# ScalarE's order in a state-space loop, and where the loop's preparation stands, in a two-layer hybrid decoder step

## The reference, cut to what matters

```python
def s5_mixer(n, x0_re, x0_im, a_re, a_im, log_dt, b_re, b_im, c_re, c_im, d, w_glu):
    dt = jnp.exp(log_dt)[:, None]
    mag = jnp.exp(a_re * dt)
    lr = mag * jnp.cos(a_im * dt)
    li = mag * jnp.sin(a_im * dt)
    ...
    cr = ((lr - 1.0) * a_re + li * a_im) / den
    ci = (li * a_re - (lr - 1.0) * a_im) / den
    bbr, bbi = cr * b_re - ci * b_im, cr * b_im + ci * b_re
    ...
    _, _, xr, xi = lax.associative_scan(s5_combine, (ar, ai, bur, bui), axis=0)
    y = Re(C x) + d * n
    zg = jnp.einsum('bld,dz->blz', jax.nn.gelu(y), w_glu)
    return zg[..., :D_MODEL] * jax.nn.sigmoid(zg[..., D_MODEL:]), xr[-1], xi[-1]

def channel_mixer(h, g, w_up, w_down):
    a = jax.nn.relu(jnp.einsum('bld,df->blf', rmsnorm(h, g), w_up))
    return jnp.einsum('blf,fd->bld', a * a, w_down)
```

## Time and profile before

| | us |
|---|---|
| median of 3 executions | 1099.26 (1097.96 to 1101.6) |
| the profiled execution | 1100.49 |
| its span | 1098.8, mean granted TensorE clock 0.946 |
| TensorE (PE) busy | 1043.7 (95%) |
| VectorE (DVE) busy | 551.4 (50%) |
| ScalarE (ACT) busy | 414.5 (38%) |
| GpSimd (POOL) busy | 138.1 (13%) |
| up projection of layer 0 | 446 to 556 |
| state-space loop | 739 to 797 |
| gated projection | 797 to 851 |

### The profile page before, as it was taken

The page is one execution under the profiler, slowest core; times in us unless marked ns, Lnnn a source line. Parts: engine busy times, 40 slices in busy tenths (PEclk is TensorE's granted clock), DMA queues, the critical chain, the costliest instruction groups (busy, mean ns, idle before and its releaser), DMA issues.

```text
span 1098.8 us, 16432 instructions
## 1 busy us (share of the span) xinstructions
PE 1043.7 (95%) x6342; PEld 872.5 (79%) x6342; DVE 551.4 (50%) x965; ACT 414.5 (38%) x711; POOL 138.1 (13%) x236
## 2 busy tenths in 40 slices
PE   6998979999999969999999999999999999999997
PEld 5997536556665537889987777778999999999997
DVE  4441675556445234398451002349665675634454
ACT  6423343343123113357341001633456555533343
POOL 3441000000014303000031001850000000000000
PEclk9998978999789979999999999999589999999999
DMA  7447001211225423434432343031034444433341
GB/s 293 163 164 294 28 1 30 76 36 34 77 92 171 152 78 125 154 129 178 154 138 98 148 153 152 2 148 55 1 137 154 154 156 174 171 153 154 154 153 44
DMA packets 33758, 135.26 MB, mean 123 GB/s; under 512 B 5257, under 2 KB 16777, under 8 KB 21010
## 3 DMA queue, kind: packets, MB, share of 16 engines
q1 hardware_dynamic: 26786, 116.71, 29.1%
q0 software_dynamic: 6896, 17.51, 4.8%
HBM read 130.04 MB, written 4.17 MB: 122 GB/s over the span
## 4 chain that ended last, share of the span: by engine, by line
PE 77%; DVE 11%; ACT 5%; issue 4%; POOLq 1%; DMA 1%; POOL 1%; DVEq 0%; ACTq 0%
PE ps L805 17%; PE ps L774 12%; PE ps L775 12%; PE ps L776 11%; PE ps L965 8%; DVE ring_split L1728 2%; PE ps L870 1%; PE ps L968 1%; PE ps L1241 1%; POOLq L609 1%; PE ps L1030 1%; PE ps L1249 1%; PE ps L1256 1%; PE ps L1255 1%; ACT glu_hi_split L1354 1%
## 5 line engine op out<-in xcount | busy, mean ns | idle before, releaser
L965 PE MATMUL ps<-arena 128*128 128x512 f32 x256 | 147.3, 667 | 0.0
L805 PE MATMUL ps<-arena,ring 128*128 128x288 f32 x512 | 124.3, 406 | 0.0
L805 PEld LDWEIGHTS ps<-arena,ring 128*128 128x128 f32 x512 | 97.2, 190 | 26.8
L968 PEld LDWEIGHTS ps<-arena 128*128 128x128 f32 x256 | 51.0, 199 | 66.2 <-issue 66.2
L774 PE MATMUL ps<-nhi_split,hi_split 128*128 128x288 f32 x320 | 95.2, 298 | 1.7 <-DVE up_lo_split L1737 1.6
L776 PE MATMUL ps<-nhi_split,ring_split 128*128 128x288 f32 x320 | 94.1, 294 | 0.0
L1728 DVE TENSOR_TENSOR ring_split<-ring,hi_split 128x2048 fp32r<-128x2048 f32 x36 | 82.2, 2286 | 23.0 <-ACT hi_split L1354 23.0
L1861 DVE TENSOR_REDUCE arena<-arena 128x8 f32<-128x512 f32 x64 | 43.5, 684 | 78.6 <-ACT arena L1429 78.6
L774 PE MATMUL ps<-up_nhi_split,up_hi_split 128*128 128x288 f32 x256 | 76.6, 299 | 4.4 <-DVE ring_split L1728 2.4
L1354 ACT ACTIVATE hi_split<-ring 128x2048 fp32r<-128x2048 f32 x36 | 68.7, 1910 | 31.4 <-PE ps L776 22.7
L2030 DVE TENSOR_TENSOR hT<-hT,ps 128x288 f32<-128x288 f32 x24 | 10.9, 453 | 132.9 <-PE ps L805 100.8
(11 more groups left out here) (377 smaller groups left out, 2343.2 us busy)
## 6 DMA issues: line engine op xcount, KB each, us to landing
ring<-in_stream SPq DMA_DIRECT2D x97, 1024.0 KB, 4.9
arena<-in_ckvT SPq DMA_DIRECT2D x64, 128.0 KB, 2.0
arena<-in_ckv POOLq DMA_DIRECT2D x49, 128.0 KB, 2.6
arena<-in_wu POOLq DMA_DIRECT2D x1, 2176.0 KB, 10.2
arena<-in_s POOLq DMA_DIRECT2D x4, 512.0 KB, 3.8
out_gla_s<-arena POOLq DMA_DIRECT2D x4, 512.0 KB, 2.9
arena<-in_ckv SPq DMA_DIRECT2D x15, 128.0 KB, 2.3
hT<-in_x SPq DMA_DIRECT2D x2, 576.0 KB, 4.5
```

The costliest lines, as they stand in the source:

```text
L805: mm = pe.matmul(ps[base:base + m, 0:T], wv[:, k, col:col + m], rhs(k), start=first and k == 0, stop=last and k == blocks - 1)
L965: mm = pe.matmul(ps[:, :], pages[:, p % 4, j, k], wuk[:, k], start=k == 0, stop=k == KB - 1)
L968: mm = pe.matmul(sc[:, 32 * j:32 * j + 32], pages[:, p % 4, j, k], qabs[:, k, b], start=False, stop=j == 1 and k == KB - 1, skip_group_che ...
```

## The change

```diff
--- before.py
+++ after.py
@@ -213,10 +213,9 @@
                 if i >= 0:
                     g.add(("y5", i), "side", 4, 4 + turn % 4)
                     turn += 1
-            for i in range(0, 8, 2):
-                for n in (i, i + 1):
-                    main(("glu_a", n))
-                    main(("glu_g", n))
+            for n in range(8):
+                main(("glu_a", n))
+                main(("glu_g", n))
         side(("ss", 1 + 3 * L))
         for i in range(FB):
             main(("up", L, i))
@@ -1276,13 +1275,11 @@
                 for name, col in (("glu_a", 0), ("glu_g", P)):
                     project_split((name, i), w, col, 256, glu_split, wait, blocks=range(lo, hi), last=hi == DB, first=lo == 0)

-            for i in range(2):
-                pe.wait_ge(glu_first, i + 1)
-                glu_pieces(i, 0, 4, split_wait(2) if i == 0 else None)
-            for i in range(2):
-                split_unit(f"glu{i}")
-                glu_pieces(i, 4, 8, split_wait(2) if i == 0 else None)
-            for i in range(2, 8):
+            pe.wait_ge(glu_first, 1)
+            glu_pieces(0, 0, 4, split_wait(2))
+            split_unit("glu0")
+            glu_pieces(0, 4, 8, split_wait(2))
+            for i in range(1, 8):
                 split_unit(f"glu{i}")
                 glu_pieces(i, 0, 8)
             mlp(1)
@@ -1548,12 +1545,12 @@
                     hi_unit(U["up0_1"])
                 if b == 5:
                     hi_unit(U["up0_2"])
-            rsqrt(rs[:, :], ("ss", 1))
             act.wait_ge(s5_angle, 1)
             act.activation(cf(4), cf(1), ACT.Exp).then_inc(s5_sin, 1)
             act.activation(cf(5), cf(2), ACT.Sin).then_inc(s5_sin, 1)
             act.activation(cf(6), cf(2), ACT.Sin, scale=0.5).then_inc(s5_sin, 1)
             table_with_exp_and_ln()
+            rsqrt(rs[:, :], ("ss", 1))
             for i in range(6):
                 squared_up(0, i)
             act.wait_ge(s5_zero, 1)
@@ -1646,19 +1643,20 @@
                 for b in range(4 * half, 4 * half + 4):
                     act.activation(glu_nhi[:, b], n3[:, b], ACT.Copy).then_inc(n_hi, 1)

-            for i in range(-2, 8):
-                if i + 2 < 8:
-                    sample_inputs(i + 2, 0)
-                    sample_inputs(i + 2, 1)
-                    sample_states(i + 2)
-                    last_states(i + 2)
-                if i >= 0:
-                    mixed(i)
-                if i == 4:
+            for i in range(10):
+                if i < 8:
+                    sample_inputs(i, 0)
+                    sample_inputs(i, 1)
+                    sample_states(i)
+                if 1 <= i < 9:
+                    last_states(i - 1)
+                if i >= 2:
+                    mixed(i - 2)
+                if i == 6:
                     n_hi_half(0)
-                if i == 5:
+                if i == 7:
                     hi_unit(U["glu0"])
-                if i == 6:
+                if i == 8:
                     hi_unit(U["glu1"])
             n_hi_half(1)
             table_with_exp_and_ln()
@@ -2046,7 +2044,7 @@
                     dve.wait_ge(a_hi, i)
                     V.tensor_tensor(a2lo[:, i - 1], a2[:, i - 1], as_whole(a2hi[:, i - 1]), ALU.subtract).then_inc(a_split, 1)

-            def gated(base, values, gates, unit_of=None, after=None, normed=False):
+            def gated(base, values, gates, unit_of=None, between=None, after=None, normed=False):

                 for i in range(8):
                     e = (tA, tB)[(base + i) % 2]
@@ -2055,6 +2053,8 @@
                         V.tensor_tensor(e, ps[:, 0:T], rs[:, :], ALU.mult).then_inc(bank_of(gates[i]), 1)
                     if unit_of:
                         lo_unit(unit_of(i))
+                    if between:
+                        between(i)
                     ps = result(dve, values[i])
                     dve.wait_ge(gate_ready, base + i + 1)
                     V.tensor_tensor(e, e, ps[:, 0:T], ALU.mult).then_inc(bank_of(values[i]), 1)
@@ -2078,7 +2078,6 @@
                     lo_unit(U["up0_2"])
                 gained_lo(1, b, prm("g_mlp0"), up_nhi, up_lo)
             add_squares(1, 2)
-            copied(dve, ("ss", 1))

             def s5_prepare():

@@ -2098,7 +2097,6 @@
                 link(V.scalar_tensor_tensor(cf(2), cf(3), -C1, cf(2), ALU.mult, ALU.add))
                 link(V.scalar_tensor_tensor(cf(2), cf(3), -C2, cf(2), ALU.mult, ALU.add))
                 V.tensor_scalar(cf(2), cf(2), 3.1415925, -3.1415925, ALU.min, ALU.max).then_inc(s5_angle, 1)
-                up(0, range(0, 1))
                 dve.wait_ge(s5_sin, 3)
                 tt(cf(6), cf(6), cf(6), ALU.mult)
                 link(V.tensor_scalar(cf(6), cf(6), -2.0, 1.0, ALU.mult, ALU.add))
@@ -2111,16 +2109,12 @@
                     tt(pr, t0, t1, ALU.subtract)
                     tt(t0, xr, xi, ALU.mult)
                     tt(pi, t0, t0, ALU.add)
-                    if pr is l2r:
-                        up(0, range(1, 2))
-                up(0, range(2, 3))
                 for i, (x, s) in enumerate(((l4r, 1.0), (l4i, -1.0), (l4i, 1.0), (l4r, 1.0))):
                     link(V.tensor_scalar(cf(16 + i), x, s, None, ALU.mult))

                 tt(t0, are, are, ALU.mult)
                 tt(t1, aim, aim, ALU.mult)
                 tt(cf(13), t0, t1, ALU.add)
-                up(0, range(3, 4))
                 link(V.reciprocal(cf(13), cf(13)))
                 link(V.tensor_scalar(cf(14), lr, -1.0, None, ALU.add))
                 tt(t0, cf(14), are, ALU.mult)
@@ -2146,7 +2140,8 @@
                 dve.wait_ge(s5raw_in, 80)
                 tt(braw[0], braw[0], g_rows, ALU.mult)
                 tt(braw[1], braw[1], g_rows, ALU.mult)
-                up(0, range(4, 5))
+                copied(dve, ("ss", 1))
+                up(0, range(0, 5))
                 cmul(cur, braw, cf(15), cf(14), b_power, range(5, 6))
                 for e in range(1, 4):
                     up(0, range(3 + 3 * e, 5 + 3 * e))
@@ -2281,12 +2276,11 @@
             lo_half(0, 0)
             for b in range(4):
                 n_lo(2, b, glu_nhi)
-            lo_half(1, 0)
             lo_half(0, 1)
             for b in range(4, DB):
                 n_lo(2, b, glu_nhi)
-            lo_half(1, 1)
-            parts[0] += 2
+            parts[0] += 1
+            lo_unit(U["glu1"])

             def final_states():

@@ -2312,15 +2306,13 @@
             def h_lo_parts(i):
                 if i:
                     dve.wait_ge(h_gated, 8 + i)
-                    if i < 7:
-                        gained_lo(3, i - 1, prm("g_mlp1"), to=up1_lo)
+                    gained_lo(3, i - 1, prm("g_mlp1"), to=up1_lo)
                 if i in (4, 6):
                     add_squares(4, i // 2 - 2)

-            gated(8, [("glu_a", i) for i in range(8)], [("glu_g", i) for i in range(8)], unit_of=lambda i: U[f"glu{i}"] + 2, after=h_lo_parts)
-            for b in (6, 7):
-                dve.wait_ge(h_gated, 8 + b + 1)
-                gained_lo(3, b, prm("g_mlp1"), to=up1_lo)
+            gated(8, [("glu_a", i) for i in range(8)], [("glu_g", i) for i in range(8)], unit_of=lambda i: U[f"glu{i}"] + 2, between=h_lo_parts)
+            dve.wait_ge(h_gated, 16)
+            gained_lo(3, 7, prm("g_mlp1"), to=up1_lo)
             add_squares(4, 2)
             lo_unit(U["up1_0"] + 2)
             copied(dve, ("ss", 4))
```

## The result

The kernel after takes 1092.38 us (1090.19 to 1094.51, 5 executions), the kernel before 1100.12 (1097.96 to 1101.6, 5): ratio 0.9943 [0.9925, 0.9961]. The ratios, with their 95% intervals, are not the quotients of the medians (1092.38 / 1100.12 = 0.9930), so both are given. The kernel is faster, as forecast, and inside the range, but by 7.7 us between the medians (6.3 by the ratio) and not by 10.3. One execution of all that follow, 1298.96 us in e7_fill at a mean clock of 0.732, was a slow one and is left out of the ratios. The profiled execution took 1092.79, span 1091.1, mean granted clock 0.950 (before 1100.49, 1098.8, 0.946).

A forecast was written before the change was run, and what follows sets the result against it. TensorE, busy for 95% of the span, was taken to bound the kernel. The terms -3.6 - 7.9 + 1.15 = -10.3 us gave 1090.2 for a profiled execution, 1089.0 on the median's scale; range 1086 to 1097.

The forecast's parts named there:

- Part 1: Layer 0's up projection: state-space preparation ahead of the first factor's evacuations cuts TensorE's waits for VectorE; -3.6 us.
- 0.1 of restart each: Layer 0's up projection: some 0.1 us of TensorE restart saved with each wait that goes.
- Part 2: State-space loop: ScalarE's new order removes waits and the clock falls only near 774; -7.9 us.
- the wait on the samples: State-space loop: VectorE's 0.78 us wait for ScalarE's samples was to go.
- Rival (a): State-space loop: the clock still falls near 764, total gain only 3.5 us, 1095.7; chance 0.18.
- Part 3: Gated projection: unit 0 before unit 1, h's low parts ahead of the product; a loss of +1.15 us.
- The chain's own arithmetic: Gated projection: the serial ScalarE-VectorE chain takes 5.9 + 0.43 us a unit, with h's low part in it.
- the first gate: Gated projection: ready earlier because unit 0 finishes first, ending VectorE's 0.71 us wait; -0.6 us.
- longer than 1.63: Start of layer 1's first factor: TensorE's wait above 1.63 us was a sign that the forecast is right.

The follow-up runs named there:

- e7_fill: The change as made plus 3, 4 and 3 unread matmuls in TensorE's waits of the loop's last three output blocks; median 1092.92 us, ratio 0.9939.
- e2: The kernel before with only ScalarE's new order in the state-space loop; median 1096.7 us, ratio 0.9963.
- e4: The kernel before with the early preparation and the new loop order, without the gated projection's edits; median 1090.11 us, ratio 0.9888.
- e5: The change as made, unchanged, run again; median 1094.96 us, ratio 0.9952 to the kernel before.
- e6: The change as made, with h's low part moved ahead of the weight unit's low part; median 1090.17 us, ratio 0.9918 to before.
- e9: The change as made, but with h's low parts behind the addition, as in the kernel before; median 1092.46 us, ratio 0.9928 to before.
- e10: The change as made, but with the old unit order in the gated projection; median 1095.14 us, ratio 0.9953 to before.
- e12_before: The kernel before, unchanged, profiled a second time; one execution, 1098.22 us.
- e3_gated: The kernel before with only the gated projection's edits (unit order, h's low parts ahead of the product); median 1101.81 us, ratio 1.0013.
- e1_prep: The kernel before with only the state-space preparation moved ahead of layer 0's first evacuations; median 1102.35 us, ratio 1.0017.
- e8_both: The change as made, with h's low part ahead of the unit's and the unread filler matmuls; median 1086.38 us, ratio 0.9886 to before.

## Why the prediction was right or wrong

**Part 1: mechanism right, -3.6 mis-sized.** It measured -4.29 in its stage in all profiles that have it. The preparation ended 12.0 us behind its start (451.44 to 463.48), as forecast (449.2 to 461.2), and the first wait shrank from 1.48 to 1.19 (forecast 1.28). TensorE's waits fell by 3.3, forecast 3.1. What was too small is the 0.1 of restart each: 4.29 - 3.3 leaves 1.0 for four waits gone, about 0.25 each. The starts of before's matmuls show it: at the wait of 0.55 us the starts are 0.84 apart and the next start follows 0.24 later, where 0.13 is the usual distance. The table load took 1.28 us and the next operation began 0.01 behind it, and the preparation ended as the row had it, not 1.4 us later. By the Trainium skill, ScalarE: Activation LUTs, "What ACT_TABLE_LOAD costs", a drain of about 1.38 us comes with each switch; it doesn't show in this trace.

**Part 2: right for the profile, wrong for the kernel.** The step that failed is the base of the -7.9: the low clock from 764 on the earlier trace rows is charged to the kernel before as if every execution had it, and only some do. Against that profile -7.9 was forecast and -7.98 measured, with the clock up to 774, the wait on the samples gone and VectorE at 5.39 us a block, as written. But in the commoner course before takes 235.7, and the new order is worth 235.74 - 233.90 = 1.8 us. That is nearly what VectorE waited for the samples there, 0.78 and 0.91 us, and no longer waits in after; the low clock at the loop's end is 17.1 us long in both. The order also seems to be steadier: all seven profiles with it and without fillers (after, e2, e4, e5, e6, e9, e10) had 233.9. Of the small waits, the 0.31 went and the 1.08 became 0.71 (forecast 0.6). By the Trainium skill, TensorE: Matmul & The Clock Gate, "A second HAM failure mode: psum-queue depth-cycling", frequent short idle times of TensorE between groups of matmuls let the clock go down and up. The trace of before agrees; that of e12_before, with the same waits, held 1.00 through them. Rival (a), a fall near 764 in the kernel after, didn't come about.

**Part 3: mis-sized, +1.15 against +0.79 and then +1.43.** The chain's own arithmetic held: a period of 6.33 us, forecast 5.9 + 0.43, and the first gate without its wait (800.23). TensorE restarts 58.3 us behind the projection's start, forecast 58.7. Against e12_before, with its restart at 57.37, that is +0.95, nearer to the +1.15. What the sum lacked was the step after it: the wait at layer 1's first factor grew from 1.63 to 2.93 (0.79 by the later restart, 0.5 because TensorE came there sooner, 52.8 us behind the projection's start and not 53.3: its low clock ended about 3.5 us behind that start and not 4.5), and at its end the clock fell: +1.43. I had named "longer than 1.63" as a sign and charged nothing for what follows. Part 3 in all cost 2.2 us in after and 2.9 in e5_again; nearly all of the difference, 0.6 us, is the wait for VectorE's product at line 2060 some 270 us behind the projection's start, 0.32 and 0.95 us. What moves that wait stays open.

**The sum.** The projection started 9.9 us earlier (forecast 11.5), 12.3 without the +2.35. Against the profile on record: +2.35 (not the change's), -4.29, -7.98, +0.79, +1.43 = -7.7. Against the commoner course of before: -4.33 - 1.84 + 2.37 = -3.8 by the profiles of after and e12_before. The medians of e5_again's run have 1094.96 - 1098.05 = -3.1, its ratio of 0.9952 about -5.3; executions of before with either course are in them. So of the 10.3 us forecast, 6.1 hung on the course of the clock in one execution. It is partly luck that the measured gain came so near to it: the commoner course gives a gain that is in the range only because the range took in rival (a), whose reason, an early fall in the kernel after, didn't hold.

## What to carry to other kernels

Where a forecast is built on a stretch of low clock, look whether the mean clocks and the spread of the other executions are those of the profiled one (a second profile says more), and price the stage with the other course too; compare stages, not whole times. Price each longer wait of TensorE twice, once for itself and once for a clock that may fall with it. A short piece of work that must go somewhere in a serial chain belongs where its engine waits for the chain (h's low part, placed there, turned a loss of 2 to 3 us into a gain of 2).

## What was not expected of the hardware

Short waits of TensorE between dense 288-column products can come with the low clock: it fell within about 1 us of the end of waits of 1.75 (e2_loop), 2.63 (e3_gated), 2.93 (after), 3.25 (e10_between) and 3.28 us (e7_fill), and not at 1.34 (e9_units) and 1.63 (before). The same 0.90, 0.31 and 1.08 us in the loop were followed by it in before and e1_prep, and not in e3_gated and e12_before. And the clock's course in the mixers of layer 0, which no edit touched, moved the start of the up projection by up to 12.9 us (443.86 to 456.77), more than the 11.7 us between the medians of before and e8_both.
